# Two-block decoder on one core: weight splits ahead of the new tile's parts, and ScalarE squaring the tiles of the second block's first norm

## The chip, the cores and the metric

One core of a Trainium2 chip runs the whole program as a single launch. The metric is the device time of that launch in microseconds (us), as the median of several runs; less is better.

## The reference, cut to what matters

The reference is a decoder in fp32 for 256 tokens of width 2048: one pooling layer, one layer of sparse attention, a norm, and then a second block with three kinds of attention and a feed-forward part. What the change touches is what stands between a residual sum and the projections behind it:

```python
return x + jnp.concatenate([y_nsa, y_mem], axis=-1) @ w_out   # "wo1": x becomes the layer's output
...
x = first_block(...)            # ends with rmsnorm(h, final_g)
h = rmsnorm_2(x, attn_norm[l])  # the second block's first norm, of a tensor that has just been normed
qkv = jnp.einsum('bsd,de->bse', h, w_qkv[l])
...
x = x + jnp.einsum('bse,ed->bsd', y, w_o[l])                  # "wo2"
h = rmsnorm_2(x, ffn_norm[l])
```

The kernel takes the two norms in a row as one. For that it needs two sums over the 2048 channels of every token: of x squared, and of (x times final_g) squared.

## The kernel before, in words

Activations lie transposed: the residual `M.X` is 16 tiles (j = 0 to 15) of 128 channels by 256 tokens. Every weight is streamed once from HBM, in 699 **units** of at most 128x1024 numbers. A matmul of fp32 numbers is made of fp32r products: ScalarE rounds a unit to its high part (`s_wh`, line 1050), VectorE subtracts to get the low part (`s_wl`, line 1572), and TensorE multiplies both. These two steps are the **split** of a unit. On every engine's program `nxt()` stands for one unit: it lets the side tasks (attention heads and the like) advance by one step and then issues the split. The split of unit k+3 waits until TensorE has finished unit k (three buffers, `NR`), and SyncE loads a unit into one of four staging buffers when VectorE has split the unit four before it.

A **residual stage** is the output projection that is added to `M.X`: `wo0` (first layer), `wo1` (second layer), `wo2` (second block's attention) and `wd` twice (feed-forward). A tile of the wo stages has two units. For the first `early` tiles (4 in wo0, 8 in wo1, 12 in wo2) TensorE does the first unit of each tile, then the second unit of each, as there are late inputs; the tiles behind them have both units in a row. After each unit or tile VectorE adds the product to `M.X` (`add`, lines 1798 and 1800). When a tile is complete, `post(j)` makes its **parts** for the next matmuls: ScalarE the high part (`high`, line 1062), VectorE the low part (`low`, line 1590), and GpSimd its share of the sum of squares. GpSimd has two scratch tiles (`PSQ`) and one accumulator per sum (`ACC`).

Each engine executes its own instructions strictly in the order written here; waits are on semaphores. Behind wo1, TensorE starts the group `qc` (four tiles: their four first units, then their four second ones). Between the fourth and the fifth unit stands `eff_hook`: it waits until both sums have all 16 tiles (`sqc1`, `sqc2`) and then does the two matmuls with ones that add them over the channels (line 578). The same norm is used two more times, one unit and two units later (`eff_norms`, lines 587 and 578). ScalarE and VectorE turn the result into a reciprocal root (lines 1067, 1069 and 1596 to 1600).

GpSimd's next work behind the sums of wo1 is `late()`: eight small scalings, a cast (line 2366) that waits for the table `con3`, and an addition over 128x2048 numbers into the bias table `s_bt` (line 2370). SyncE issues the loads of both tables behind the weight unit that is eight behind the last of wo1.

Of the kernel before, what the change touches and what calls it, by code (L numbers as in the profile page):

```python
# [11 lines left out]
ALU = mybir.AluOpType  # L12
ACT = mybir.ActivationFunctionType
# [4 lines left out]
KT = 16  # L18
# [1018 lines left out]
def scalar_program(e, S, P, M):  # L1037
    w, side, done = Waits(e, S), Side(), [0]
# [13 lines left out]
    def nxt(n=1):  # L1052
        for _ in range(n):
            side.tick()
            split()
# [4 lines left out]
    def high(R, j, src, gain, name):  # L1060

        e.activation(R[:, 0, j, :], src, ACT.Copy, scale=gain).then_inc(S[name + "h"], 1)
# [221 lines left out]

    def square(n):
        w.wait_ge("l2_o", n + 1)
        w.wait_ge("z_d", 32)
        if n >= 2:
            w.wait_ge("hn_mm", n - 1)
        e.activation(M.ZT[n % 2][:, :], M.PSO[n % 2][:, 0:T], ACT.Square).then_inc(S["hn_sq"], 1)  # L1290

    def head_rsqrt(n, dim, eps):
# [112 lines left out]
    def residual(name, post, order=2, early=4, units=2):  # L1405
        for n in range(order):
            for j in range(early):
                if n == order - 1:
                    post(j)
                nxt()  # L1410
        for j in range(early, KT):
            nxt(units - 1)
            post(j)
            nxt()


    tables()
# [74 lines left out]
    def post_c(j):  # L1492
        w.wait_ge(*P.out["wo1", j])
        w.wait_ge("gfa", 1)
        w.wait_ge("units", P.end["zm", 1, 3])
        high(M.RY, j, M.X[:, j, :], M.GFA[:, j:j + 1], "hc")

    residual("wo1", post_c, early=8)

# [28 lines left out]
    for hv in range(2):  # L1528
# [14 lines left out]
        def post(j, hv=hv):  # L1543
            if hv:
                side.start(times_g(j))
# [15 lines left out]
def vector_program(e, S, P, M):  # L1561
    w, side, done, chained = Waits(e, S), Side(), [0], [0]
# [11 lines left out]
    def nxt(n=1):  # L1574
        for _ in range(n):
            side.tick()
            split()
# [33 lines left out]
    def whole(t):  # L1611
        w.wait_ge("units", P.end[t])
        return M.product(P.bank[t])
# [181 lines left out]
    def add(t, j):  # L1795

        b = whole(t)
        chain(e.tensor_tensor(M.X[:, j, :], b[:, T:2 * T], M.X[:, j, :], ALU.add))  # L1798
        link()
        e.tensor_tensor(M.X[:, j, :], b[:, 0:T], M.X[:, j, :], ALU.add).then_inc(S["out"], 1)  # L1800

    def residual(name, post, order=(0, 1), early=4, units=2, begin=None):
        for n, m in enumerate(order):
            for j in range(early):
                last = n == len(order) - 1
                if n == 0 and begin:
                    begin(j)
                if n:
                    w.wait_ge(*P.out[name, "part", order[n - 1], j])
                add((name, j) if last else (name, "part", m, j), j)  # L1810
                if last:
                    post(j)
                nxt()
        for j in range(early, KT):
            nxt(units - 1)
            if begin:
                begin(j)
            add((name, j), j)
            post(j)
            nxt()  # L1820

    def kv_norm():
        yield
# [389 lines left out]
    for hv in range(2):  # L2213
# [25 lines left out]
        def post(j, hv=hv):  # L2239
            if hv and j == KT - 1:  # L2240
                w.wait_ge(*P.out[("wd", 1), j])
                w.wait_ge("y_lo", 48)
                e.tensor_tensor(M.YT[0][:, :], M.X[:, j, :], M.X[:, j, :], ALU.mult).then_inc(S["sq15"], 1)
# [4 lines left out]
    for n, (a, b) in enumerate(((0, 1), (1, 3), (3, 6), (6, 9), (9, 11))):  # L2248
        w.wait_ge("xg", b)
        for j in range(a, b):  # L2250
            x = e.tensor_tensor(M.X[:, j, :], M.X[:, j, :], M.RB[1][:, :], ALU.mult)
# [3 lines left out]
def pool_program(e, S, P, M):  # L2255
    w, side, chained = Waits(e, S), Side(), [0]
# [6 lines left out]
    def chain(ins):  # L2263

        ins.then_inc(S["pool"], 1)
        chained[0] += 1

    def link():
        w.wait_ge("pool", chained[0])

    squared = [0]

    def square(acc, j, src, name):

        if j == 0:
            e.tensor_tensor(acc, src, src, ALU.mult).then_inc(S[name], 1)
            return
        b = M.PSQ[squared[0] % 2][:, :]
        squared[0] += 1
        chain(e.tensor_tensor(b, src, src, ALU.mult))  # L2280
        link()
        w.wait_ge(name, j)
        e.tensor_tensor(acc, acc, b, ALU.add).then_inc(S[name], 1)  # L2283
# [200 lines left out]
        side.start(mem_head(1, j))  # L2484

    def post_c(j):
        x = M.X[:, j, :]
        w.wait_ge(*P.out["wo1", j])
        if j:
            w.wait_ge("sqc2", j)  # L2490
        square(M.ACC[0][:, :], j, x, "sqc1")
        b, b2 = M.PSQ[squared[0] % 2][:, :], M.PSQ[(squared[0] + 1) % 2][:, :]
        squared[0] += 2
        chain(e.tensor_scalar(b, x, M.vec("fing", j), None, ALU.mult))  # L2494
        link()
        if j == 0:
            e.tensor_tensor(M.ACC[1][:, :], b, b, ALU.mult).then_inc(S["sqc2"], 1)
            return
        chain(e.tensor_tensor(b2, b, b, ALU.mult))
        link()  # L2500
        e.tensor_tensor(M.ACC[1][:, :], M.ACC[1][:, :], b2, ALU.add).then_inc(S["sqc2"], 1)  # L2501
    residual(post_c, early=8)


# [40 lines left out]
    for a, b in ((11, 12), (12, 14), (14, 16)):  # L2545
        w.wait_ge("xg", b)
        for j in range(a, b):
            x = e.tensor_tensor(M.X[:, j, :], M.X[:, j, :], M.RB[1][:, :], ALU.mult)
# [162 lines left out]
```

## Time and profile before

| what | value |
|---|---|
| median of 3 runs | 2118.11 us (2116.64 to 2118.48) |
| the profiled execution's own time | 2117.76 us |
| its span in the profile | 2116.0 us |
| busy: TensorE, VectorE, ScalarE, GpSimd | 98%, 69%, 48%, 24% of the span |
| mean granted clock of TensorE | 0.991 of full speed |
| moved from HBM | 365.97 MB read, 174 GB/s over the span |

In the rows further down PE is TensorE, DVE is VectorE, ACT is ScalarE, POOL is GpSimd and SPq is SyncE's DMA queue. A row of the timeline gives the start in us, the duration in us, the engine, the line of the kernel, the operation, output <- inputs with their shapes, the number of instructions merged in the row, and in brackets the idle time ahead of it with what ended it. A row of the windows gives the stretch and its length, then the busy time of PE, PE's weight loads, DVE, ACT and POOL with their counts, then the granted clock of TensorE (1.00 is 2.4 GHz, 0.50 is 1.2 GHz), the DMA share and GB/s. Line 510 is the low-part matmul of a tile's last k-step; TensorE executes it once per tile or part, always one matmul before the end of the unit, so the distance between two such rows is a number of whole units.

### The profile page before, as it was taken

Reading aid. Unit: us, or ns where it says so; the run is one execution under the profiler, and the core shown is the slowest. Engines: PE = TensorE matmul, PEld = TensorE weight load, DVE = VectorE, ACT = ScalarE, POOL = GpSimd, SP = SyncE. Lnnn points to the kernel's source line nnn. Section 1 sums busy time; section 2 is a strip of 40 time slices with the busy share of each in tenths; the row PEclk is TensorE's granted clock in tenths of the full one; section 3 lists DMA queues with packets and bytes.
Section 4 is the critical chain, followed back from the end, with each engine's and each line's share of the span. In section 5 each row is a group of like instructions: output and inputs, shape, how many; then the busy total and the mean of one; then the engine's idle time right before and its main releaser. Section 6 shows DMA issues by size and latency. Waiting matters only on the chain.

```text
span 2116.0 us, 29531 instructions
## 1 busy us (share of the span) xinstructions
PE 2063.7 (98%) x11608; PEld 1775.0 (84%) x11608; DVE 1465.3 (69%) x2054; ACT 1008.4 (48%) x1476; POOL 509.3 (24%) x487
## 2 busy tenths in 40 slices
PE   7999999999999999989999999999999999999997
PEld 6788888888888888778877888888888888888886
DVE  8866777689786556767645677677776557777755
ACT  5545444455633554433545554455444344444443
POOL 8205542200000344790221222211010001101122
PEclk9999999999999999999999999999999999999998
DMA  7564565656754333555454445565566666556664
GB/s 247 171 187 151 184 189 189 189 191 213 220 184 146 117 105 120 169 185 179 155 164 132 147 154 160 176 192 186 188 190 183 185 190 190 188 184 193 179 187 134
DMA packets 104090, 369.99 MB, mean 175 GB/s; under 512 B 11632, under 2 KB 12944, under 8 KB 103824
## 3 DMA queue, kind: packets, MB, share of 16 engines
q1 hardware_dynamic: 103952, 368.11, 55.6%
q8 instruction: 92, 1.51, 0.3%
q14 instruction: 46, 0.38, 0.1%
HBM read 365.97 MB, written 2.10 MB: 174 GB/s over the span
## 4 chain that ended last, share of the span: by engine, by line
PE 88%; DVE 5%; POOL 4%; issue 2%; ACT 1%; DMA 0%; DVEq 0%; SPq 0%; POOLq 0%; ACTq 0%
PE psg L511 47%; PE psg L513 23%; PE psg L558 2%; PE psg L560 2%; PE psg L559 2%; DVE s_wl L1572 2%; PE psg L510 2%; PE pst L511 1%; ACT s_wh L1050 1%; POOL s_psq L2494 1%; POOL s_acc L2501 1%; POOL s_psq L2280 1%; PE pst L595 1%; DVE s_rh L1590 1%; DVE s_ry L1590 1%
## 5 line engine op out<-in xcount | busy, mean ns | idle before, releaser
L1572 DVE TENSOR_TENSOR s_wl<-s_stage,s_wh 128x1024 fp32r<-128x1024 f32 (+3 forms) x699 | 870.2, 1246 | 380.7 <-ACT s_wh L1050 378.0
L1050 ACT ACTIVATE s_wh<-s_stage 128x1024 fp32r<-128x1024 f32 (+3 forms) x699 | 727.3, 1042 | 673.6 <-PE psg L511 361.7
L511 PE MATMUL psg<-s_ry,s_wh 128*128 128x512 f32 x2672 | 943.1, 398 | 3.3 <-DVE s_mv L1639 2.5
L513 PE MATMUL psg<-s_ry,s_wl 128*128 128x256 f32 x2501 | 707.6, 283 | 0.0
L511 PEld LDWEIGHTS psg<-s_ry,s_wh 128*128 128x128 f32 x2672 | 493.6, 188 | 112.2 <-issue 3.5
L511 PE MATMUL psg<-s_rh,s_wh 128*128 128x512 f32 x1280 | 460.5, 401 | 19.7 <-DVE s_rh L1590 10.5
L513 PEld LDWEIGHTS psg<-s_ry,s_wl 128*128 128x128 f32 x2501 | 471.4, 188 | 7.7
L513 PE MATMUL psg<-s_rh,s_wl 128*128 128x256 f32 x1180 | 334.6, 284 | 0.0
L511 PEld LDWEIGHTS psg<-s_rh,s_wh 128*128 128x128 f32 x1280 | 238.6, 189 | 74.6 <-issue 10.5
L511 PE MATMUL psg<-s_hid,s_wh 128*128 128x512 f32 x704 | 244.6, 394 | 0.0
L513 PEld LDWEIGHTS psg<-s_rh,s_wl 128*128 128x128 f32 x1180 | 223.6, 190 | 2.9
L2410 POOL TENSOR_TENSOR s_hid<-s_hh,s_hid 128x256 fp32r<-128x256 f32 x44 | 53.0, 1205 | 571.4 <-ACT s_hid L1395 571.4
L513 PE MATMUL psg<-s_hid,s_wl 128*128 128x256 f32 x664 | 187.4, 282 | 0.0
L511 PEld LDWEIGHTS psg<-s_hid,s_wh 128*128 128x128 f32 x704 | 129.6, 188 | 27.1
L513 PEld LDWEIGHTS psg<-s_hid,s_wl 128*128 128x128 f32 x664 | 124.8, 188 | 2.0
L2280 POOL TENSOR_TENSOR s_psq<-s_x 128x256 f32<-128x256 f32 x74 | 59.5, 805 | 167.6 <-DVE s_x L1800 165.6
L2283 POOL TENSOR_TENSOR s_acc<-s_acc,s_psq 128x256 f32<-128x256 f32 x89 | 92.5, 1039 | 7.0
L2287 POOL TENSOR_SCALAR s_bsc<-s_bsc,s_stat 128x256 f32<-128x256 f32 (+1 forms) x56 | 44.2, 805 | 194.1 <-DVE s_stat L1950 181.7
L2292 POOL TENSOR_TENSOR s_rh<-s_yt,s_rh 128x256 fp32r<-128x256 f32 x32 | 43.0, 1345 | 117.7 <-ACT s_rh L1090 117.7
L1798 DVE TENSOR_TENSOR s_x<-psg,s_x 128x256 f32<-128x256 f32 x112 | 47.3, 422 | 34.1 <-PE psg L511 33.5
L558 PE MATMUL psg<-s_wh,s_ry 128*128 128x512 f32 x160 | 65.0, 406 | 3.6 <-DVE s_kcc L1624 1.3
L2287 POOL TENSOR_SCALAR s_csc<-s_csc,s_stat 128x128 f32<-128x128 f32 (+1 forms) x32 | 34.8, 1100 | 123.5 <-DVE s_stat L1993 110.4
(388 smaller groups left out, 2268.6 us busy)
## 6 DMA issues: line engine op xcount, KB each, us to landing
s_stage<-in_wo SPq DMA_DIRECT2D x96, 512.0 KB, 3.5
s_stage<-in_wg SPq DMA_DIRECT2D x88, 512.0 KB, 3.5
s_stage<-in_wu SPq DMA_DIRECT2D x88, 512.0 KB, 3.8
s_stage<-in_ain SPq DMA_DIRECT2D x64, 512.0 KB, 3.6
s_stage<-in_wd SPq DMA_DIRECT2D x64, 448.0 KB, 3.5
s_stage<-in_wkv SPq DMA_DIRECT2D x32, 512.0 KB, 4.0
s_stage<-in_wd SPq DMA_DIRECT2D x32, 512.0 KB, 3.6
s_stage<-in_bq SPq DMA_DIRECT2D x24, 512.0 KB, 3.6
```

Of the source, the lines that this page charges most:

```text
L510: e.matmul(o[:, T:2 * T], M.WL[:, r, ws], xh, start=False, stop=False)
L511: m = e.matmul(o, M.WH[:, r, ws], xx, start=begin, stop=end)
L513: m = e.matmul(o[:, T:2 * T], M.WL[:, r, ws], xh, start=False, stop=False)
L558: e.matmul(o[:, :], xh[:, ts], M.WH[:, r, ws], start=(k == 0), stop=False)
L1050: e.activation(M.WH[:, c % NR, 0:n], M.ST[:, c % NS, 0:n], ACT.Copy).then_inc(S["wh"], 1)
L1572: e.tensor_tensor(M.WL[:, c % NR, 0:n], M.ST[:, c % NS, 0:n], M.WH[:, c % NR, 0:n], ALU.subtract).then_inc(S["wl"], 1)
L1798: chain(e.tensor_tensor(M.X[:, j, :], b[:, T:2 * T], M.X[:, j, :], ALU.add))
L2280: chain(e.tensor_tensor(b, src, src, ALU.mult))
L2283: e.tensor_tensor(acc, acc, b, ALU.add).then_inc(S[name], 1)
L2287: x = e.tensor_scalar(ap, ap, scale, None, ALU.mult)
L2292: e.tensor_tensor(R[:, 1, j, :], M.YT[y % 2][:, :], R[:, 0, j, :].bitcast(F32), ALU.subtract).then_inc(S["y_lo"], 1)
L2410: e.tensor_tensor(M.HID[:, 1, i, :], M.HH[j % 2][:, :], M.HID[:, 0, i, :].bitcast(F32), ALU.subtract).then_inc(S["hidl"], 1)
```

## The change

Two edits. First, in the residual stages the split of a unit now comes ahead of `post(j)` on ScalarE and on VectorE: in the early zone `nxt()` then `post(j)`; behind it ScalarE does both splits and then the parts, and VectorE does split, add, split, parts. Second, in wo1 ScalarE makes both squares of a tile (into `PSQ` and into `ZT`, two buffers each) right behind the high part, and GpSimd only adds them to the two accumulators.

```diff
     # ScalarE's program
     def residual(name, post, order=2, early=4, units=2):
         for n in range(order):
             for j in range(early):
+                nxt()
                 if n == order - 1:
                     post(j)
-                nxt()
         for j in range(early, KT):
-            nxt(units - 1)
+            nxt(units)
             post(j)
-            nxt()
...
     def post_c(j):
...
         high(M.RY, j, M.X[:, j, :], M.GFA[:, j:j + 1], "hc")
+        w.wait_ge("sqk", KT)
+        w.wait_ge("z_d", 32)
+        if j >= 2:
+            w.wait_ge("sqc1", j - 1)
+            w.wait_ge("sqc2", j - 1)
+        e.activation(M.PSQ[j % 2][:, :], M.X[:, j, :], ACT.Square).then_inc(S["sqp"], 1)
+        e.activation(M.ZT[j % 2][:, :], M.X[:, j, :], ACT.Square, scale=M.vec("fing", j)).then_inc(S["sqg"], 1)
...
     # VectorE's program, residual()
                 add((name, j) if last else (name, "part", m, j), j)
+                nxt()
                 if last:
                     post(j)
-                nxt()
...
             add((name, j), j)
+            nxt()
             post(j)
-            nxt()
...
     # GpSimd's program
     def post_c(j):
-        x = M.X[:, j, :]
-        w.wait_ge(*P.out["wo1", j])
-        if j:
-            w.wait_ge("sqc2", j)
-        square(M.ACC[0][:, :], j, x, "sqc1")
-        b, b2 = M.PSQ[squared[0] % 2][:, :], M.PSQ[(squared[0] + 1) % 2][:, :]
-        squared[0] += 2
-        chain(e.tensor_scalar(b, x, M.vec("fing", j), None, ALU.mult))
-        link()
-        if j == 0:
-            e.tensor_tensor(M.ACC[1][:, :], b, b, ALU.mult).then_inc(S["sqc2"], 1)
-            return
-        chain(e.tensor_tensor(b2, b, b, ALU.mult))
-        link()
-        e.tensor_tensor(M.ACC[1][:, :], M.ACC[1][:, :], b2, ALU.add).then_inc(S["sqc2"], 1)
+
+        for acc, src, made, name in ((M.ACC[0], M.PSQ, "sqp", "sqc1"), (M.ACC[1], M.ZT, "sqg", "sqc2")):
+            w.wait_ge(made, j + 1)
+            if j == 0:
+                e.tensor_copy(acc[:, :], src[0][:, :]).then_inc(S[name], 1)
+            else:
+                w.wait_ge(name, j)
+                e.tensor_tensor(acc[:, :], acc[:, :], src[j % 2][:, :], ALU.add).then_inc(S[name], 1)
```

How the instructions now stand, at three places. The changed file has other line numbers on VectorE and GpSimd: 1572 is 1579 there, 1590 is 1597, 1798 and 1800 are 1805 and 1807.

VectorE in wo1, at the first tile that is complete, before:

```order
L1798 TENSOR_TENSOR s_x<-psg,s_x 128x256
L1800 TENSOR_TENSOR s_x<-psg,s_x 128x256
L1590 SCALAR_TENSOR_TENSOR s_ry<-s_x,s_gfa,s_ry 128x256
L1572 TENSOR_TENSOR s_wl<-s_stage,s_wh 128x1024
L1798 TENSOR_TENSOR s_x<-psg,s_x 128x256
```

The same place in the changed kernel:

```order
L1805 TENSOR_TENSOR s_x<-psg,s_x 128x256
L1807 TENSOR_TENSOR s_x<-psg,s_x 128x256
L1579 TENSOR_TENSOR s_wl<-s_stage,s_wh 128x1024
L1597 SCALAR_TENSOR_TENSOR s_ry<-s_x,s_gfa,s_ry 128x256
L1805 TENSOR_TENSOR s_x<-psg,s_x 128x256
```

The split (output `s_wl`) has moved from behind the low part (output `s_ry`) to between the addition and the low part. The pattern repeats for each early tile, and is the same in wo0 and wo2.

ScalarE in wo1 at the first complete tiles, before:

```order
L1090 ACTIVATE s_rh<-s_yt 128x256
L1050 ACTIVATE s_wh<-s_stage 128x1024 x2
L1062 ACTIVATE s_ry<-s_x,s_gfa 128x256
L1050 ACTIVATE s_wh<-s_stage 128x1024
L1062 ACTIVATE s_ry<-s_x,s_gfa 128x256
```

And in the changed kernel:

```order
L1090 ACTIVATE s_rh<-s_yt 128x256
L1050 ACTIVATE s_wh<-s_stage 128x1024 x3
L1062 ACTIVATE s_ry<-s_x,s_gfa 128x256
L1502 ACTIVATE s_psq<-s_x 128x256
L1503 ACTIVATE s_zt<-s_x,s_vec 128x256
L1050 ACTIVATE s_wh<-s_stage 128x1024
L1062 ACTIVATE s_ry<-s_x,s_gfa 128x256
```

One more split (output `s_wh`) stands ahead of the first high part, and two squares (lines 1502 and 1503) follow each high part. No table load is added on ScalarE.

GpSimd in wo1, its work for one tile, before:

```order
L2280 TENSOR_TENSOR s_psq<-s_x 128x256
L2283 TENSOR_TENSOR s_acc<-s_acc,s_psq 128x256
L2494 TENSOR_SCALAR s_psq<-s_x,s_vec 128x256
L2499 TENSOR_TENSOR s_psq<-s_psq 128x256
L2501 TENSOR_TENSOR s_acc<-s_acc,s_psq 128x256
```

In the changed kernel, its first three tiles:

```order
L2498 COPY s_acc<-s_psq 128x256
L2498 COPY s_acc<-s_zt 128x256
L2501 TENSOR_TENSOR s_acc<-s_acc,s_psq 128x256
L2501 TENSOR_TENSOR s_acc<-s_acc,s_zt 128x256
L2501 TENSOR_TENSOR s_acc<-s_acc,s_psq 128x256
L2501 TENSOR_TENSOR s_acc<-s_acc,s_zt 128x256
```

Five instructions per tile became two.

## Rows read from the trace of the kernel before

**Rows 1.** The page: busy time of each engine.

```profile
PE 2063.7 (98%) x11608; PEld 1775.0 (84%) x11608; DVE 1465.3 (69%) x2054; ACT 1008.4 (48%) x1476; POOL 509.3 (24%) x487
```

**Rows 2.** Timeline of PE, line 510: wo0, wo1, behind its hook, wo2.

```profile
339.94 0.27 PE L510 MATMUL psg<-s_ry,s_wl 128*128 128x256 f32 x1
...
357.50 0.28 PE L510 MATMUL psg<-s_ry,s_wl 128*128 128x256 f32 x1
...
865.29 0.27 PE L510 MATMUL psg<-s_rh,s_wl 128*128 128x256 f32 x1
...
895.07 0.28 PE L510 MATMUL psg<-s_rh,s_wl 128*128 128x256 f32 x1
...
923.17 0.28 PE L510 MATMUL psg<-s_rh,s_wl 128*128 128x256 f32 x1
...
948.28 0.27 PE L510 MATMUL psg<-s_ry,s_wl 128*128 128x256 f32 x1
...
951.97 0.28 PE L510 MATMUL psg<-s_ry,s_wl 128*128 128x256 f32 x1
...
955.21 0.27 PE L510 MATMUL pst<-s_ry,s_wl 128*128 128x256 f32 x1
...
1298.46 0.27 PE L510 MATMUL psg<-s_rh,s_wl 128*128 128x256 f32 x1
...
1358.41 0.28 PE L510 MATMUL psg<-s_rh,s_wl 128*128 128x256 f32 x1
```

**Rows 3.** Timeline of DVE: one early tile of wo2.

```profile
1303.08 0.42 DVE L1800 TENSOR_TENSOR s_x<-psg,s_x 128x256 f32<-128x256 f32 x1
1304.08 0.49 DVE L1590 SCALAR_TENSOR_TENSOR s_ry<-s_x,s_vec,s_ry 128x256 fp32r<-128x256 f32 x1 [0.58 <-ACT s_ry L1062]
1305.03 1.23 DVE L1572 TENSOR_TENSOR s_wl<-s_stage,s_wh 128x1024 fp32r<-128x1024 f32 x1 [0.46 <-ACT s_wh L1050]
...
1306.62 0.42 DVE L1800 TENSOR_TENSOR s_x<-psg,s_x 128x256 f32<-128x256 f32 x1
```

**Rows 4.** Timeline of ACT: the same tile.

```profile
1303.54 0.51 ACT L1062 ACTIVATE s_ry<-s_x,s_vec 128x256 fp32r<-128x256 f32 x1 [2.09 <-DVE s_x L1800]
1303.95 1.04 ACT L1050 ACTIVATE s_wh<-s_stage 128x1024 fp32r<-128x1024 f32 x1
```

**Rows 5.** Timeline of POOL in wo1: its first, one middle and its last instruction.

```profile
855.62 0.61 POOL L2276 TENSOR_TENSOR s_acc<-s_x 128x256 f32<-128x256 f32 x1 [7.30 <-DVE s_x L1800]
...
920.98 1.59 POOL L2501 TENSOR_TENSOR s_acc<-s_acc,s_psq 128x256 f32<-128x256 f32 x1
...
942.00 0.72 POOL L2501 TENSOR_TENSOR s_acc<-s_acc,s_psq 128x256 f32<-128x256 f32 x1
```

**Rows 6.** Timeline of PE: the first matmul of the hook behind wo1.

```profile
942.83 1.19 PE L578 MATMUL pso<-s_acc,s_one 128*128 128x256 f32 x2 [7.91 <-issue]
```

**Rows 7.** Windows, behind an early wait and behind the hook's wait.

```profile
70.20:73.30 3.10, 3.10 (x12) 2.62 (x11) 1.67 (x6) 0.00 (x0) 0.00 (x0) 0.50 0.76 276
942.80:947.20 4.40, 4.37 (x12) 3.65 (x13) 1.26 (x4) 1.84 (x3) 4.15 (x9) 0.50 0.01 3
```

**Rows 8.** Waits of PE: us in total, times, longest; two of them.

```profile
PE psg L511 <- DVE s_mv L1639: 2.5, 1, 2.5
...
PE psg L558 <- DVE s_kcc L1624: 1.3, 1, 1.3
```

**Rows 9.** Timeline of SPq, POOL and DVE behind the hook: table and bias addition.

```profile
933.07 0.43 SPq L2591 DMA_DIRECT2D s_csc<-in_con  x1
...
947.13 1.55 DVE L1572 TENSOR_TENSOR s_wl<-s_stage,s_wh 128x1024 fp32r<-128x1024 f32 x1
...
947.57 5.56 POOL L2370 TENSOR_TENSOR s_bt<-s_bt,s_csc 128x2048 f32<-128x2048 f32 x1
...
949.62 3.79 DVE L1626 SCALAR_TENSOR_TENSOR s_qc<-s_qc,s_rb 128x256 f32<-128x256 f32 x1
```

**Rows 10.** DMA issues of that stretch: KB each, median us to landing.

```profile
s_csc<-in_con SPq DMA_DIRECT2D x1, 320.0 KB, 9.1
```

More of the change, by code:

```diff
@@ L1286, in square @@
         w.wait_ge("l2_o", n + 1)
-        w.wait_ge("z_d", 32)
         if n >= 2:
             w.wait_ge("hn_mm", n - 1)
+        else:
+            w.wait_ge("sqc2", KT)
         e.activation(M.ZT[n % 2][:, :], M.PSO[n % 2][:, 0:T], ACT.Square).then_inc(S["hn_sq"], 1)
@@ L2486, in post_c @@
     def post_c(j):
-        x = M.X[:, j, :]
-        w.wait_ge(*P.out["wo1", j])
-        if j:
-            w.wait_ge("sqc2", j)
-        square(M.ACC[0][:, :], j, x, "sqc1")
-        b, b2 = M.PSQ[squared[0] % 2][:, :], M.PSQ[(squared[0] + 1) % 2][:, :]
-        squared[0] += 2
-        chain(e.tensor_scalar(b, x, M.vec("fing", j), None, ALU.mult))
-        link()
-        if j == 0:
-            e.tensor_tensor(M.ACC[1][:, :], b, b, ALU.mult).then_inc(S["sqc2"], 1)
-            return
-        chain(e.tensor_tensor(b2, b, b, ALU.mult))
-        link()
-        e.tensor_tensor(M.ACC[1][:, :], M.ACC[1][:, :], b2, ALU.add).then_inc(S["sqc2"], 1)
+        for acc, src, made, name in ((M.ACC[0], M.PSQ, "sqp", "sqc1"), (M.ACC[1], M.ZT, "sqg", "sqc2")):
+            w.wait_ge(made, j + 1)
+            if j == 0:
+                e.tensor_copy(acc[:, :], src[0][:, :]).then_inc(S[name], 1)
+            else:
+                w.wait_ge(name, j)
+                e.tensor_tensor(acc[:, :], acc[:, :], src[j % 2][:, :], ALU.add).then_inc(S[name], 1)
     residual(post_c, early=8)
```

## The prediction

> **What bounds the kernel now.** I read the page first: TensorE is busy for 98% of the span, VectorE for 69%, GpSimd for 24% [rows 1]. So only what makes TensorE wait, or run slowly, can be won back, and the page alone hides it, because a matmul that is held up is stretched in the records and counts as busy. I therefore measured TensorE by the distance between its line-510 matmuls, which is a whole number of units. At its own pace a unit takes 2.81 us: from 895.07 to 923.17 are 10 units, 28.10 us [rows 2]. Against that ruler four places are late:
>
> - wo0, 339.94 to 357.50: 6 units, 17.56 us instead of 16.86, late by 0.70.
> - wo1, 865.29 to 895.07: 9 units, 29.78 instead of 25.29, late by 4.49.
> - wo2, 1298.46 to 1358.41: 19 units, 59.95 instead of 53.39, late by 6.56.
> - the hook behind wo1, 923.17 to 948.28: 5 units (14.05) and the hook's two matmuls. One such matmul costs 0.43: 951.97 to 955.21 is 3.24, a unit and one matmul. So 14.91 would do, 25.11 were taken: late by 10.20 [rows 2].
>
> The timelines say why. In an early tile VectorE adds (two instructions), sits idle 0.58 for ScalarE's high part, does the low part, sits idle 0.46 for the split that ScalarE did only behind the high part, and splits. A tile comes every 3.54 us (1303.08 to 1306.62), although VectorE works only 0.42 + 0.42 + 0.49 + 1.23 = 2.56 of it [rows 3]. ScalarE spends 2.09 idle and 1.55 busy [rows 4]. It is a ring of waits, with no engine full. The splits are some units ahead when a zone begins, which is worth 1.5 us: in wo2 eleven intervals of 3.54 exceed TensorE's by 11 x 0.73 = 8.0, and 6.56 were lost.
>
> The hook is another matter. GpSimd needs from 855.62 to 942.72 for the sums of 16 tiles, 5.4 us each, with an instruction of 0.61 to 0.72 alone and up to 1.59 in company [rows 5], while a tile leaves TensorE every 2.81 or 5.62. It ends 0.1 us ahead of the hook's first matmul, which had waited 7.91 [rows 6]. And behind that idle time the granted clock is 0.50, its 1.2 GHz level, for 4.40 us [rows 7]: half of these, 2.2, is the rest of the 10.20.
>
> **The change part by part.**
>
> 1. Split ahead of the parts. VectorE's order becomes add, split, low. ScalarE's split now waits only for TensorE, and runs while VectorE adds; the high part runs while VectorE splits. Both idle times of the ring close, and VectorE's work of 2.56 per early tile fits under 2.81. TensorE is the bound again. What is later by it are the parts, by one split (1.23) at most; they are for the group behind the stage, whose second half needs the last of them more than 11 us (four units) later, so this costs nothing. Saved: 0.70 + 4.49 + 6.56 = 11.75. At wd TensorE keeps its pace, and only ScalarE's final scalings move by a unit: 0.
>
> 2. ScalarE's squares. Not in the trace in this form; the nearest row is the high part, same shape and engine, 0.51 [rows 4]. Per early tile of wo1: 1.04 + 3 x 0.51 = 2.57, below 2.81; later tiles 3.6 of 5.62. The bounds: 0.4 and 0.6 each give 2.4 and 2.8, both fit. I take 0. If they did not fit, each 0.1 over would cost 8 x 0.1, less the 1.5 of lead. Behind the waiting square on ScalarE stands the split of the next unit, for which VectorE and then TensorE wait.
>
> 3. GpSimd's two additions. 0.72 each alone, 1.59 each in company [rows 5]: 1.4 to 3.2 per tile where it was 5.4. At 3.2 it falls behind the 2.81 of the early tiles by 0.4 x 7 = 2.8, and two buffers and the 5.62 tiles take that in. After the last tile it needs one high part, two squares and two additions, some 4 to 5 us; the hook stands four units, 11.2 us, behind. The wait is gone with 6 us to spare, and with it the slow clock. Saved: 10.20.
>
> 4. What is late next. With GpSimd free early, its bias addition runs as soon as its tables are there. The split that releases the table's load comes 4.49 earlier: issue 933.07 - 4.49 = 928.6, landing 9.1 later [rows 9, 10], 937.7; the cast some 0.5, so the addition starts at 938.2. It shows 5.56, of which its start, 947.57 to 948.68, lies under a split of VectorE: 4.45 alone. A VectorE instruction with two inputs from the same memory stood through it: 3.79 where its like takes 0.49 [rows 3, 9]. Before, that fell into the time that TensorE's stall had given away. Now: the hook starts at about 934.8 - 4.5 = 930.3. Until the fifth unit behind it, TensorE has 0.86 of the hook, four units (11.24), 0.88 for the column sums (948.28 to 951.97 less a unit) and 0.43 [rows 2]: it wants that unit at 943.7. VectorE is held until 938.2 + 4.45 = 942.7, then has the rest of its instruction (0.3), three small ones (0.42 each) and the split (1.23) [rows 3] and a signal of 0.1 to 0.2: 945.7. Wait: 2.0. Is the clock halved behind that? Behind the wait of 2.5 it was 0.50 for the 3.10 us of the window, behind those of 1.3 nothing is late [rows 7, 8]; 2.0 is nearer to 2.5, so I add half of 3.1, 1.6. Bounds: 0 (the table lands when VectorE can spare it) and 5.56 + 2.2. I take 3.6.
>
> The sum: 11.75 + 10.20 - 3.6 = 18.35. The profiled execution took 2117.76 (span 2116.0): 2099.4. It stands 0.35 below the median, so I say **2099.8**, 0.86% less.
>
> **A price for the memory port.** The row that shows a cost is the 3.79 [rows 9]. The Trainium skill, "SBUF — State Buffer", section "SBUF: two separate sides", says that VectorE with two SBUF inputs and a GpSimd instruction that reads SBUF exclude each other for a whole instruction. By that rule, which speaks against closing the ring, the time is that of rival B, 2101.1, since splits and low parts could not overlap GpSimd at all; by the rows alone it is 2099.8.
>
> **The rivals.**
>
> - A, the bias addition costs nothing: it lands in spare time, or VectorE is further ahead than I have it. For it: TensorE runs from 951.97 to 955.21 with no loss right under the 3.79. Against it: there it had been given 10 us. Time 2118.1 - 21.95 = 2096.2.
> - B, VectorE and GpSimd take turns in the early zones. Split, low part, square and addition do not overlap: 1.23 + 0.49 + 0.61 + 0.72 = 3.05 per tile [rows 3, 5], 0.24 over TensorE's. In wo2 11 x 0.24 = 2.6 less the lead of 1.5 costs 1.1, in wo1 0.2. For it: an addition of 1.59. Against it: VectorE's additions from the product take 0.84 per tile in which GpSimd can have the memory, and the lead grows as the split is earlier. Time 2101.1; with a longer wait at the bias addition up to 2104.5.
> - C, the ring closes only in part, because the parts or the additions hold the product's buffers and so TensorE: half of the 11.75 remains, 2105.7.
> - D, slower: the handshake on wo1's two square buffers. ScalarE's square of tile j waits for GpSimd's additions of tile j-2, and its splits stand behind. If GpSimd took P per tile, TensorE would be paced by P. The gain of 18.35 and 4.2 more are eaten if 16 tiles take 22.6 + 1.5 longer than the 67.4 of their 24 units: P above 5.7, so 2.9 per addition where the longest row has 1.59. Time 2122 at that point. That the change does nothing is excluded by the orders of instructions; the same time would need P about 5.4.
>
> **How the numbers follow.** The forecast (2097.5 to 2101.5) 0.45; A 0.23; B and a dearer bias addition 0.22; C 0.05; D and no change 0.05. From 2095.3, a little below A, to 2104.5, the end of B, lie 0.88 less what spills over the edges. What tells a change here from none is 0.2%, 4.2 us; only D and the edge of C are not faster: faster 0.94, same 0.03, slower 0.03.
>
> **What would show it.** Step 1: line-510 distances of 2.81 or 5.62 throughout wo0, wo1 and wo2, and VectorE's additions 2.81 apart. Step 2: squares of 0.4 to 0.6, no long idle time of ScalarE ended by GpSimd. Step 3: GpSimd's last addition of wo1 some 5 us behind the last tile, no idle time at the first line-578 matmul, clock 1.00 there. Step 4: a VectorE instruction of 3 to 4.5 us under the bias addition and a TensorE gap of about 2 us within four to six units of the hook. The prediction is wrong if line-510 distances stay above 2.9 in the early zones, if ScalarE waits for GpSimd tile after tile, or if a new stall appears behind wo1 that the profile before has no sign of.

## The result and the profile after

The changed kernel takes **2096.06 us** (median of 4 runs, 2095.16 to 2096.87), beside 2117.41 (4 runs, 2116.64 to 2118.48) for the kernel before on the same chip: ratio 0.9901, 95% interval 0.9889 to 0.9912. The forecast was 2099.8 with a range of 2095.3 to 2104.5. The profiled execution took 2095.29 us, its span is 2093.5 us.

The page after, busy time of each engine, to be read against [rows 1]:

```profile
PE 2056.4 (98%) x11608; PEld 1771.4 (85%) x11608; DVE 1482.3 (71%) x2054; ACT 1022.6 (49%) x1508; POOL 483.1 (23%) x441
```

ScalarE has 32 more instructions and GpSimd 46 fewer; TensorE's share still says nothing. The ruler does. Line 510 of TensorE in the changed kernel, in wo1 and in wo2, where [rows 2] were late by 4.49 and 6.56:

```profile
865.20 0.27 PE L510 MATMUL psg<-s_rh,s_wl 128*128 128x256 f32 x1
870.82 0.27 PE L510 MATMUL psg<-s_rh,s_wl 128*128 128x256 f32 x1
...
915.78 0.28 PE L510 MATMUL psg<-s_rh,s_wl 128*128 128x256 f32 x1
...
1296.54 0.27 PE L510 MATMUL psg<-s_rh,s_wl 128*128 128x256 f32 x1
...
1313.42 0.27 PE L510 MATMUL psg<-s_rh,s_wl 128*128 128x256 f32 x1
```

From 865.20 to 915.78 are 18 units in 50.58 us, from 1296.54 to 1313.42 six units in 16.88: 2.81 each, and so through all of wo0, wo1 and wo2. The ring is gone. VectorE, ScalarE and GpSimd at one early tile of wo2, to be read against [rows 3, 4]:

```profile
1305.77 0.41 DVE L1805 TENSOR_TENSOR s_x<-psg,s_x 128x256 f32<-128x256 f32 x1
...
1306.68 1.23 DVE L1579 TENSOR_TENSOR s_wl<-s_stage,s_wh 128x1024 fp32r<-128x1024 f32 x1
1307.82 0.83 DVE L1597 SCALAR_TENSOR_TENSOR s_ry<-s_x,s_vec,s_ry 128x256 fp32r<-128x256 f32 x1
1308.58 0.41 DVE L1805 TENSOR_TENSOR s_x<-psg,s_x 128x256 f32<-128x256 f32 x1
```
```profile
1308.40 1.06 ACT L1050 ACTIVATE s_wh<-s_stage 128x1024 fp32r<-128x1024 f32 x1 [1.22 <-PE psg L511]
```
```profile
1306.72 1.66 POOL L2287 TENSOR_TENSOR s_psq<-s_x 128x256 f32<-128x256 f32 x1 [0.27 <-DVE s_x L1807]
```

VectorE's additions stand 2.81 apart (1305.77, 1308.58), and ScalarE's split waits for TensorE and for nothing else. VectorE has no idle time left in these rows. GpSimd's square begins beside VectorE's split (1306.72 and 1306.68) and takes 1.66, where its like takes 0.61 alone; the low part behind the split takes 0.83, where it was 0.49. The two engines hold each other up, and since VectorE's additions still keep TensorE's 2.81, there is just room for it.

The hook behind wo1 [rows 6]: TensorE's rows from the last of wo1 to the end of the late places, GpSimd's last sum and its next work, and VectorE under the bias addition.

```profile
927.37 0.59 PE L578 MATMUL pso<-s_acc,s_one 128*128 128x256 f32 x2
...
930.68 0.28 PE L510 MATMUL psg<-s_ry,s_wl 128*128 128x256 f32 x1
...
937.62 0.27 PE L510 MATMUL pst<-s_ry,s_wl 128*128 128x256 f32 x1
...
939.07 0.51 PE L511 MATMUL pst<-s_ry,s_wh 128*128 128x512 f32 x1 [0.94 <-DVE s_wl L1579]
...
941.63 0.28 PE L510 MATMUL pst<-s_ry,s_wl 128*128 128x256 f32 x1
...
942.61 0.47 PE L511 MATMUL psg<-s_ry,s_wh 128*128 128x512 f32 x1 [0.47 <-DVE s_wl L1579]
...
947.96 0.28 PE L510 MATMUL psg<-s_ry,s_wl 128*128 128x256 f32 x1
```
```profile
919.28 0.92 POOL L2501 TENSOR_TENSOR s_acc<-s_acc,s_zt 128x256 f32<-128x256 f32 x1
920.18 5.74 POOL L2368 TENSOR_SCALAR s_ids<-s_cons 128x128 bf16<-128x128 f32 x8
932.63 0.66 POOL L2373 CAST s_ddb<-s_csc 128x384 bf16<-128x384 f32 x1 [6.71 <-DMA s_csc<-in_con]
933.26 4.60 POOL L2377 TENSOR_TENSOR s_bt<-s_bt,s_csc 128x2048 f32<-128x2048 f32 x1
```
```profile
933.34 4.54 DVE L1607 SCALAR_TENSOR_TENSOR s_rc<-s_cw,s_rc 128x2 f32<-128x2 f32 x1
937.80 1.21 DVE L1579 TENSOR_TENSOR s_wl<-s_stage,s_wh 128x1024 fp32r<-128x1024 f32 x1
```

From 915.78 to 930.68 are 14.90 us where 25.11 were, and the first matmul at line 578 has no idle time ahead of it; GpSimd was done at 920.20, 7.2 us before. Then TensorE is late by 1.20 (937.62 to 941.63, less 2.81) and 0.71 (941.63 to 947.96, less 5.62): 1.91. The reason is the row of VectorE at 933.34: an instruction over two columns stands for 4.54 us, as long as GpSimd's bias addition beside it. The windows behind the hook and over the waits:

```profile
927.00:931.00 4.00, 4.00 (x24) 3.55 (x23) 1.69 (x5) 2.02 (x4) 0.00 (x0) 1.00 1.02 424
938.00:946.00 8.00, 6.59 (x36) 5.47 (x36) 7.83 (x13) 2.36 (x3) 0.00 (x0) 1.00 0.40 131
```

The granted clock is 1.00 in both.

**Where the 22.5 us between the two profiled executions are.** wo0 0.70, wo1 4.47, wo2 6.52, the hook 10.21, the waits behind it -1.61 (1.91 now, where the kernel before lost 0.30 at the same unit), a place in the first layer 1.6, the start-up 0.6. The place in the first layer is none of the change's. It is a group of 48 matmuls of 15 columns; its row and the window around it, before and then after:

```profile
656.44 6.57 PE L736 MATMUL pss<-s_kcmp,s_qn 128*128 128x15 f32 x48
```
```profile
655.00:672.00 17.00, 17.00 (x99) 15.58 (x98) 10.65 (x26) 3.78 (x5) 0.00 (x0) 0.80 0.34 100
```
```profile
655.12 5.51 PE L736 MATMUL pss<-s_kcmp,s_qn 128*128 128x15 f32 x48
```
```profile
655.00:672.00 17.00, 17.00 (x107) 15.47 (x106) 10.64 (x25) 4.84 (x6) 0.00 (x0) 0.90 0.44 130
```

The clock falls to half in every profiled execution around this group though TensorE never idles there, and for longer in some: 0.90 of 17 us is 3.4 us at half clock, 0.80 is 6.8, which is 1.7 or 3.4 us of lost work. The kernels below show the same at the same code: 0.90 in the profiled runs of e1, e6, e7, e9 and e11, 0.80 in those of e2, e3, e4, e8 and e10, and 0.70, 10.2 us at half clock, in that of e5. Runs of one kernel differ by about as much: the changed kernel's four are two of 2095.2 to 2095.3 with a mean clock of 0.996 and two of 2096.8 to 2096.9 with 0.994.

### The profile page after: what moved, and what is told of

The parts are those of the page before. It is cut to its first block, busy times and chain, and to the rows that moved or that the text cites. A ratio compares the mean times of both kernels' runs of the same rounds, so it can differ in the third digit from the quotient of the medians.

```text
span 2093.5 us, 29532 instructions
## 1 busy us (share of the span) xinstructions
PE 2056.4 (98%) x11608; PEld 1771.4 (85%) x11608; DVE 1482.3 (71%) x2054; ACT 1022.6 (49%) x1508; POOL 483.1 (23%) x441
## 4 chain that ended last, share of the span: by engine, by line
PE 94%; DVE 4%; issue 0%; ACT 0%; DMA 0%; DVEq 0%; SPq 0%; ACTq 0%
PE psg L511 51%; PE psg L513 25%; PE psg L558 2%; PE psg L560 2%; PE psg L559 2%; PE psg L510 2%; DVE s_wl L1579 2%; PE pst L511 1%; PE pst L595 1%; DVE s_rh L1597 1%; PE pst L513 1%; DVE s_ry L1597 1%; PE pss L759 1%; PE pso L779 0%; PE pst L683 0%; PE pst L684 0%
## 5 line engine op out<-in xcount | busy, mean ns | idle before, releaser
L2290 POOL TENSOR_TENSOR s_acc<-s_acc,s_psq 128x256 f32<-128x256 f32 x74 | 85.8, 1160 | 5.8
```

## The experiments

All are compared with the kernel before, run on the same chip (median 2116.5 to 2117.7). "Interval" is the distance of two line-510 matmuls in an early zone. The change has one more edit than the two that are told above: the tiles `ZT` also serve ScalarE's later squares of the heads, and the first two of those now wait for the sums of wo1 (`sqc2`) instead of `z_d`. e1 is without it, all the others have it; in the trace of the changed kernel no wait of ScalarE at those squares is ended by GpSimd.

**e1, the new order alone.** The kernel before with the diff's first part only; GpSimd does all five instructions per tile.

```diff
 # VectorE, residual(), against before (ScalarE likewise); both post_c as before
+                nxt()
                 if last:
                     post(j)
-                nxt()
... (and the same behind the early tiles)
```

> The kernel before with the new order of split and parts alone; GpSimd still makes both squares of wo1. My theory (two waits in series): wo0 gives back 0.7 us and wo2 6.6 us, but the 4.5 us won in wo1 are lost again at the hook, because GpSimd's chain of 5.4 us per tile ends at the same time whatever TensorE does; the idle time at the first line-578 matmul grows from 7.9 to about 12 us. Total 2117.4 - 7.3 = 2110.1 us. Rival (the savings simply add): 2117.4 - 11.75 = 2105.7 us.

Measured 2105.19 us (2104.52 to 2106.59), ratio 0.9944 (0.9927 to 0.9960). My 2110.1 was wrong and the additive rival's 2105.7 nearly right. The zones run at 2.81. The hook, which I had supposed to wait for all that TensorE gains ahead of it, waits only 1 us more than before. TensorE, and then GpSimd in e1 and in the kernel before:

```profile
936.12 1.19 PE L578 MATMUL pso<-s_acc,s_one 128*128 128x256 f32 x2 [8.90 <-issue]
```
```profile
931.34 0.72 POOL L2500 TENSOR_TENSOR s_acc<-s_acc,s_psq 128x256 f32<-128x256 f32 x1
...
935.29 0.72 POOL L2500 TENSOR_TENSOR s_acc<-s_acc,s_psq 128x256 f32<-128x256 f32 x1
```
```profile
938.05 0.72 POOL L2501 TENSOR_TENSOR s_acc<-s_acc,s_psq 128x256 f32<-128x256 f32 x1
```

GpSimd's chain started earlier with TensorE, and it became faster too: from its first instruction (852.39) to 936.0 are 83.6 us where it was 87.1 [rows 5], 5.2 per tile instead of 5.4. The pace of a tile isn't fixed. The last one takes 3.95 us in both kernels (931.34 to 935.29; before, 938.05 to 942.00 [rows 5]), while most of those behind the early zone take 5.6 in both. Of the 3.5 us gained, 1.8 lie in the last three tiles: 5.6, 4.0 and 4.0 in e1, 6.7, 4.8 and 4.0 before. The likely reason is that VectorE's work for wo1 is over at an earlier tile of GpSimd's; no run isolates it.

**e2, the squares alone.** The changed kernel with both engines' old order.

```diff
 # ScalarE, residual(), against the changed kernel (VectorE likewise)
-                nxt()
                 if n == order - 1:
                     post(j)
+                nxt()
...
-            nxt(units)
+            nxt(units - 1)
             post(j)
+            nxt()
```

> The changed kernel with the old order of split and parts, so that only the squares have moved to ScalarE. My theory: the wait at the hook and the slow clock go (10.2 us), the bias addition costs 1.6 of it, and the ring of waits in wo1 becomes longer by the two squares that now stand between the high part and the split on ScalarE (0.7 us per early tile, 7 tiles, 4.9 us): 2117.4 - 10.2 + 1.6 + 4.9 = 2113.7 us; the interval of VectorE's additions in wo1's early zone goes from 3.55 to about 4.25 us. Rival (savings simply add, the ring stays at 3.55): 2108.8 us.

Measured 2113.16 us (10 runs, 2111.7 to 2114.1), ratio 0.9981 (0.9972 to 0.9990): as I expected, and not the 2108.8 of the additive rival. In wo1 TensorE is paced at 4.25 us per tile, slower than before:

```profile
866.44 0.28 PE L510 MATMUL psg<-s_rh,s_wl 128*128 128x256 f32 x1
870.68 0.28 PE L510 MATMUL psg<-s_rh,s_wl 128*128 128x256 f32 x1
```
```profile
870.32 1.23 DVE L1580 TENSOR_TENSOR s_wl<-s_stage,s_wh 128x1024 fp32r<-128x1024 f32 x1 [1.17 <-ACT s_wh L1050]
```

VectorE now idles 1.17 ahead of its split where it was 0.46 [rows 3]: the squares lengthen the ring by 0.71, since ScalarE's split stands behind them. So the squares are hidden in the changed kernel only because the split stands ahead of them; together the two edits give more than their sum, 21.4 us where e1 has 12.3 and e2 4.3. Behind the hook TensorE waited once, for 1.64 us, and the clock stayed at 1.00.

**e4, only ScalarE's order** (VectorE keeps add, low, split; squares as in the changed kernel).

```diff
 # VectorE, residual(), against the changed kernel
-                nxt()
                 if last:
                     post(j)
+                nxt()
... (and the same behind the early tiles)
```

> The changed kernel with VectorE's old order (add, low part, split); ScalarE keeps split, high part, squares. My theory: the ring of waits is half open: VectorE waits 0.2 to 0.6 us per early tile for the high part and not for the split, an interval of about 2.9 to 3.1 us against TensorE's 2.81; less the lead this costs 0 to 2 us in wo2 and about 0.5 us in wo1: 2096 to 2098.5 us. Rival (only VectorE's order matters, since the split must reach TensorE through it): the early zones fall back to 3.5 us per tile, 2107 us.

Measured 2106.10 us (2105.17 to 2108.49), ratio 0.9947 (0.9933 to 0.9962). My 2096 to 2098.5 was wrong; the rival's number, 2107, held, but not its reason, that only VectorE's order matters: e5 below has VectorE's new order alone and is slower still. The interval is 3.53, although ScalarE's split is done in time. Against e2, which has neither engine's new order, that is still 7.1 us less. VectorE in wo2:

```profile
1309.22 0.48 DVE L1597 SCALAR_TENSOR_TENSOR s_ry<-s_x,s_vec,s_ry 128x256 fp32r<-128x256 f32 x1 [0.58 <-ACT s_ry L1062]
1309.62 1.76 DVE L1579 TENSOR_TENSOR s_wl<-s_stage,s_wh 128x1024 fp32r<-128x1024 f32 x1
```

Of the two idle times the 0.46 is gone, but the split now takes 1.76 instead of 1.23. GpSimd's addition stands beside its start. That is 0.53 given back in another form, which raised the question that the next run answers.

**e9, the same without GpSimd in wo2.** The kernel leaves out the sum of squares behind wo2.

```diff
-        square(M.ACC[0][:, :], j, M.X[:, j, :], "sqf")
+        if j == 0:
+            square(M.ACC[0][:, :], j, M.X[:, j, :], "sqf")
+        else:
+            w.wait_ge("sqf", j)
+            e.tensor_tensor(M.ACC[0][:, 0:2], M.ACC[0][:, 0:2], M.X[:, j, 0:2], ALU.add).then_inc(S["sqf"], 1)
```

> ScalarE's new order alone, VectorE's old one (add, low, split), and in wo2 GpSimd's square and addition of 128x256 numbers per tile replaced by one addition of 128x2 from the second tile on (so that the sum of squares behind wo2, and with it the output, is left out). With full squares this order gave an interval of 3.54 us, and VectorE's split took 1.76 us instead of 1.23 while GpSimd added. My theory: those 0.53 us are VectorE waiting for the memory that GpSimd holds; without GpSimd the interval in wo2 is 0.42 + 0.42 + 0.58 idle + 0.49 + 1.23, less some overlap, 3.0 us, wo2 loses some 0.8 us instead of 6.56, and the time is 2106.1 - 5.8 = 2100.3 us; wo1 stays at 3.53. Rival: the split is held by something of ScalarE or TensorE, and GpSimd only stands beside it: the interval stays 3.54 and the time 2106.

Measured 2100.85 us (2098.87 to 2102.92), ratio 0.9924 (0.9911 to 0.9938), 5.3 less than e4 where I had said 5.8.

```profile
1308.88 0.49 DVE L1597 SCALAR_TENSOR_TENSOR s_ry<-s_x,s_vec,s_ry 128x256 fp32r<-128x256 f32 x1 [0.58 <-ACT s_ry L1062]
1309.28 1.22 DVE L1579 TENSOR_TENSOR s_wl<-s_stage,s_wh 128x1024 fp32r<-128x1024 f32 x1
...
1311.87 0.48 DVE L1597 SCALAR_TENSOR_TENSOR s_ry<-s_x,s_vec,s_ry 128x256 fp32r<-128x256 f32 x1 [0.58 <-ACT s_ry L1062]
```

The split is back at 1.22, and the low parts stand 2.99 apart instead of 3.53. So the 0.53 were VectorE waiting for the memory that GpSimd held. The interval of 2.9 to 3.1 that I had expected of e4 is there once GpSimd is out of the way, and the lead nearly covers it: TensorE's matmuls stay 2.81 apart in wo2 until the last early tile and lose 0.3 us in all.

**e5, only VectorE's order** (ScalarE keeps parts, then split).

```diff
 # ScalarE, residual(), against the changed kernel
-                nxt()
                 if n == order - 1:
                     post(j)
+                nxt()
... (and the same behind the early tiles)
```

> The changed kernel with ScalarE's old order (high part, squares, split); VectorE keeps add, split, low part. My theory: the ring is longer than in the kernel before, as VectorE's split now waits for the addition, the high part and ScalarE's split in series and the low part stands behind it: 0.85 + 0.45 + 1.05 + 1.2 + 0.4 = about 4.0 us per early tile in wo0 and wo2 and 4.7 us in wo1. Loss against the changed kernel: wo2 11 x 1.2 - 1.5 = 11.6, wo1 7 x 1.9 - 1.5 = 11.8, wo0 3 x 1.2 - 1.5 = 2.1: about 2121 us, slower than the kernel before. Rival (the order on either engine gives half of the gain): 2107 us.

Measured 2123.47 us (8 runs, 2121.89 to 2125.02), ratio 1.0028 (1.0018 to 1.0039): slower than before, as expected. Interval 3.94 in wo0 and wo2, 4.64 in wo1 (I had 4.0 and 4.7). VectorE in wo2:

```profile
1308.29 1.23 DVE L1580 TENSOR_TENSOR s_wl<-s_stage,s_wh 128x1024 fp32r<-128x1024 f32 x1 [1.53 <-ACT s_wh L1050]
```

This half of the edit makes a longer ring: add, high part, split, VectorE's split, add.

**e6, one square ahead instead of two.**

```diff
-            w.wait_ge("sqc1", j - 1)
-            w.wait_ge("sqc2", j - 1)
+            w.wait_ge("sqc1", j)
+            w.wait_ge("sqc2", j)
```

> The changed kernel in which ScalarE's squares of tile j wait for GpSimd's additions of tile j-1, as if there were one buffer of each kind. My theory: GpSimd's additions end 0.6 us ahead of the next tile's square, so the handshake has room and nothing changes, 2096.1 us. Rival (the handshake is near its limit, and the second buffer is what hides it): ScalarE waits in the early zone, up to 0.5 us per tile less the lead, 2098 us or more.

Measured 2095.60 us (2094.89 to 2097.07), ratio 0.9901: no change. Rival D's handshake has room even at half its depth.

**e7, GpSimd's work doubled in wo1.**

```diff
                 w.wait_ge(name, j)
+                spare = M.ET[0 if name == "sqc1" else 1]
+                e.tensor_tensor(spare[:, :], src[j % 2][:, :], src[j % 2][:, :], ALU.add)
                 e.tensor_tensor(acc[:, :], acc[:, :], src[j % 2][:, :], ALU.add).then_inc(S[name], 1)
```

> The changed kernel with two more additions of the same kind by GpSimd for each tile of wo1 from the second one on (into a scratch tile that nobody reads), four instead of two. My theory: GpSimd's time per tile goes from 1.7 to 3.7 to 4.6 us, over TensorE's 2.81 in the early zone, and through the two buffers it paces ScalarE and so TensorE there; 7 x 0.9 to 1.8 less two buffers and the lead is a loss of 2 to 7 us: 2098 to 2103 us. Rival (VectorE waits for GpSimd instruction by instruction, and the time is lost there): VectorE's interval rises with every GpSimd instruction also in the later tiles, 2105 us or more. Third: GpSimd is off the path at any load that fits 5.62 us, 2096.1 us.

Measured 2095.61 us (2095.01 to 2095.93), ratio 0.9899: no change, where I had 2098 to 2103. ScalarE does wait for GpSimd, at the seventh tile for the first time:

```profile
873.32 0.42 ACT L1502 ACTIVATE s_psq<-s_x 128x256 f32<-128x256 f32 x1 [1.61 <-POOL s_acc L2503]
```

VectorE's additions are 3.0 to 3.1 apart, some 0.25 over TensorE's pace, and TensorE lost 0.14 us in all: seven tiles of 0.24 are 1.7, and the splits that were ahead took nearly all of it. That is the interval of rival B, measured in wo1, where B had priced it at 0.2. In wo2, with its eleven intervals, no run has it.

**e3, the bias addition in four pieces of 128x512.**

```diff
-        e.tensor_tensor(M.BT[:, :, :], M.BT[:, :, :], chm, ALU.add).then_inc(S["bt"], 1)
+        for q in range(4):
+            b = M.BT[:, 2 * q:2 * q + 2, :]
+            x = e.tensor_tensor(b, b, chm[:, 2 * q:2 * q + 2, :], ALU.add)
+        x.then_inc(S["bt"], 1)
```

> The changed kernel with GpSimd's bias addition over 128x2048 done in four pieces of 128x512. My theory: VectorE stood 4.5 us behind the one long instruction because GpSimd holds what both need for a whole instruction; with pieces of about 1.2 us VectorE gets in between them, the low part of the unit comes in time and the two TensorE gaps behind the hook (1.9 us together against TensorE's own pace) go: 2096.1 - 1.9 = 2094.2 us. Rival (the total that GpSimd holds it decides, not the length of one piece): VectorE is as late as before, 2096.1 us.

Measured 2095.36 us (2094.32 to 2096.73), ratio 0.9898 (0.9883 to 0.9913). VectorE at the same instruction:

```profile
933.74 1.23 DVE L1607 SCALAR_TENSOR_TENSOR s_rc<-s_cw,s_rc 128x2 f32<-128x2 f32 x1
```

It is held for one piece (1.23 instead of 4.54) and then gets in between. TensorE is late by 0.60 instead of 1.91, where I had expected nothing to be left; the 1.3 us are seen in the trace, while the median lies between my 2094.2 and the rival's 2096.1 and, 0.7 from the changed kernel's, doesn't separate the two.

**e8, the tables loaded four units earlier.** What the addition costs should depend on when it runs.

```diff
-    while issued[0] < P.end["wo1", KT - 1] + 9:
+    while issued[0] < P.end["wo1", KT - 1] + 5:
```

> The whole change, but SyncE issues the tables' loads four units (11.2 us) earlier, so that GpSimd's cast and bias addition need no longer wait for them: they start behind its eight scalings, at about 926 to 927 us instead of 933. My theory: the 1.91 us that TensorE is late behind the hook come from the moment at which the bias addition holds VectorE; at 927 VectorE is still ahead of TensorE by its full lead, the distances behind the hook become 14.90, 3.69, 3.24, 2.81 and 5.62, and the time is 2096.06 - 1.9 = 2094.2 us. Rival 1: the addition of 4.6 us takes from VectorE what it takes at any moment, and TensorE is late by 1.9 us all the same, only at another unit: 2096. Rival 2: the addition now holds the column sums and reciprocal roots behind the hook, which TensorE waits for, and more is lost: 2098.

Measured 2094.69 us (2093.81 to 2095.13), ratio 0.9893 (0.9879 to 0.9906), the fastest kernel of the study. GpSimd, VectorE and TensorE:

```profile
928.10 5.55 POOL L2377 TENSOR_TENSOR s_bt<-s_bt,s_csc 128x2048 f32<-128x2048 f32 x1
```
```profile
931.60 2.33 DVE L1605 SCALAR_TENSOR_TENSOR s_nw<-s_nw,s_rb 128x256 f32<-128x256 f32 x1
```
```profile
931.00:938.00 7.00, 7.00 (x45) 6.26 (x44) 6.68 (x10) 3.33 (x8) 2.65 (x1) 1.00 0.32 109
```

The addition now starts 5.2 us earlier in the trace, and 6.9 earlier against TensorE's matmuls of the hook. Its start lies under a split of VectorE, 1.94 us of it in a time in which VectorE waits for ScalarE, and only 1.9 are left for the instruction at 931.60. The distances behind the hook are 14.90, 3.69, 3.24, 2.81 and 5.62: nothing is late. The profiled run gained the 1.9 though it drew the longer half clock at line 736. The wait hung on the moment, as my theory had it, and both rivals are out by the distances. The medians are 1.4 apart, less than the 1.7 between runs of the changed kernel; the 1.9 rest on the trace.

**e10 and e11, the bias addition held longer.** They ask whether a longer wait at this place brings the half clock that the prediction charged, the step of it that failed.

```diff
+        held = M.BT[:, 0:4, :]      # e10; in e11 0:8, the whole table
+        chain(e.tensor_tensor(held, held, chm[:, 0:4, :], ALU.add))
+        link()
         e.tensor_tensor(M.BT[:, :, :], M.BT[:, :, :], chm, ALU.add).then_inc(S["bt"], 1)
```

> The whole change, with GpSimd's bias addition preceded by one more addition over half of the same table (128x1024, so that this half gets its mask twice). In the changed kernel the addition held VectorE for 4.60 us and TensorE was late by 1.91 us in two waits, the longer 0.94, with the clock at 1.00 behind them, where I had forecast a wait of 2.0 and half a clock. This makes the wait longer by 2.3 to 2.8. My theory (a longer wait does bring the half clock that the prediction charged, as behind the waits of 2.5 and 7.91 before): TensorE is late by 1.9 + 2.5 = 4.4 and the window behind it shows 0.50 for some 3 us, 1.5 more, 5.9 in all; time 2096.1 + 4.0 = 2100.1 us. Rival (behind the hook the clock does not fall for such waits): late by 4.4, clock 1.00, time 2098.6.

> The same with the additional addition over the whole table (128x2048, all of it gets its mask twice). My theory: TensorE is late by 1.9 + 4.6 to 5.0 = 6.6 to 6.9, then the clock is 0.50 for 3 to 4.4 us, 1.5 to 2.2 more: 8.4 in all, time 2096.1 + 6.5 = 2102.6 us. Rival (clock stays 1.00): late by 6.7, time 2100.9. Second rival: VectorE slips its splits in between the two additions and less than 5 is lost in all, time below 2099.

e10 took 2099.04 us (2098.2 to 2099.89), ratio 0.9917 (0.9903 to 0.9932); e11 2101.43 (2100.5 to 2103.51), ratio 0.9932 (0.9915 to 0.9948). Both lie between my numbers (2100.1, 2102.6) and the rival's (2098.6, 2100.9); the trace decides. TensorE's one wait in e10, and the windows behind it:

```profile
944.43 0.59 PE L511 MATMUL psg<-s_ry,s_wh 128*128 128x512 f32 x1 [3.16 <-DVE s_wl L1579]
```
```profile
944.00:946.00 2.00, 1.57 (x5) 1.40 (x6) 1.97 (x5) 0.00 (x0) 0.00 (x0) 0.66 0.30 109
946.00:948.00 2.00, 2.00 (x7) 1.64 (x7) 1.97 (x4) 0.00 (x0) 0.00 (x0) 0.50 0.46 166
```

Behind 3.16 us of waiting, TensorE runs at its 1.2 GHz level until 948. Between two line-510 matmuls that are two units apart lie 10.57 us there: 4.95 late, of which 1.8 are the half clock. e11 has waits of 0.95 and 4.14, then 0.50 again (948 to 950), and is late by 1.19 + 5.91 = 7.10. So a half clock of the size charged can follow at this place, in the one profiled execution of each; the wait was shorter than I had it (3.16 for 4.4), since VectorE does a split between the two additions.

They don't make a rule of the length. The program has a wait of 1.8 us near 31 us that the change doesn't touch. TensorE's row and the window around it, in the kernel before and in the changed one, and then in e10 the wait of 2.5 that the prediction leaned on [rows 8]:

```profile
31.17 0.50 PE L511 MATMUL psg<-s_rh,s_wh 128*128 128x512 f32 x1 [1.81 <-DVE s_wl L1572]
```
```profile
28.00:36.00 8.00, 6.08 (x25) 4.73 (x24) 8.00 (x8) 1.73 (x3) 7.68 (x9) 0.79 0.57 188
```
```profile
30.37 0.50 PE L511 MATMUL psg<-s_rh,s_wh 128*128 128x512 f32 x1 [1.79 <-DVE s_wl L1579]
```
```profile
28.00:36.00 8.00, 6.21 (x35) 5.22 (x35) 8.00 (x8) 2.92 (x4) 7.68 (x8) 1.00 0.58 197
```
```profile
68.88 0.50 PE L511 MATMUL psg<-s_ry,s_wh 128*128 128x512 f32 x1 [2.46 <-DVE s_mv L1646]
```
```profile
66.00:74.00 8.00, 5.54 (x31) 4.52 (x30) 6.92 (x11) 3.88 (x6) 3.28 (x4) 1.00 0.58 200
```

0.79 of 8 us is 3.4 us at half clock, 1.00 is none. Of the 13 profiled executions six have the half clock at the wait of 1.8 (before, e1, e3, e4, e5, e8), and ten have it at the wait of 2.5 (all but e3, e4 and e10). The same wait of the same code is followed by it in one execution and not in another.

## Why the prediction was right, step by step

The measured 2096.06 lies in the range of 2095.3 to 2104.5, but outside the forecast's own band of 2097.5 to 2101.5: the range holds it because rival A set its lower end.

**Step 1, split ahead of the parts: right, in mechanism and size.** 11.75 forecast, 11.69 measured, with VectorE's additions 2.81 apart. One engine's new order alone gives 3.53 (e4) or 3.94 (e5), so beside GpSimd's work both idle times had to go; e9 shows that without that work ScalarE's order alone would nearly do, at 2.99. VectorE's time per tile isn't the 2.56 that the prediction reckoned with but all of 2.81, since GpSimd holds it for 0.34 of them. What the prediction left open is by which wait the ring held TensorE. In the kernel before, all eight gaps of TensorE in the early zone of wo2 are of this kind:

```profile
1310.65 0.51 PE L511 MATMUL psg<-s_rh,s_wh 128*128 128x512 f32 x1 [0.45 <-DVE s_x L1800]
```

They end with VectorE's addition, which frees one of the two buffers of the product (`psg`), and not with a split. That buffer is what rival C was about; with the additions 2.81 apart it holds nothing.

**Step 2, ScalarE's squares for nothing: right.** They take 0.40 and 0.49, so an early tile costs ScalarE 2.46 where the sum had 2.57. e2 shows what the cover was worth: without the new order they cost 0.71 per tile.

**Step 3, GpSimd's two additions: right.** 10.20 forecast, 10.21 measured. They take 0.80 to 1.07 each; the time to spare was 7.2 us instead of 6.

**Step 4, the bias addition: right in place and cause, too dear by 2.** I had 3.6: a wait of 2.0 and half of 3.1 us at the slow clock. Four things differ.

- The waits come to 1.91, so that part was sized rightly, if partly by luck: the table landed sooner (issued at 925.80, cast at 932.63, 6.8 us later instead of 9.1), and the addition held VectorE from 933.3, at an earlier unit than I thought.
- The half clock didn't come. This is the step that failed: "2.0 is nearer to 2.5, so I add half of 3.1, 1.6", a clock read off the length of a wait. Behind the hook the clock stayed at 1.00 in all seven profiled executions whose longest wait there is 0.94 to 1.64 (the changed kernel, e2, e4, e5, e6, e7 and e9), and fell behind 3.16 and 4.14 (e10, e11). Nor does the length alone decide, as the waits of 1.8 and 2.5 show. The prediction leaned on one row, and passed over the wait of 1.81 with half a clock behind it in the same trace. (Behind the waits of 1.3 the clock is indeed 1.00, though rows 7 and 8 don't show it.) What decides beside the length stays open.
- I had one wait at one unit. It came as two, late by 1.20 and 0.71, with idle gaps of 0.94 and 0.47 and 3.1 us of matmuls between them. Whether the clock would have fallen behind one wait of 2.0 at this place, no run shows.
- The kernel before lost 0.30 at that unit, which I hadn't subtracted.

Priced so, the term is 1.6, and the sum 11.75 + 10.20 - 1.6 = 20.35 gives 2097.4 for the profiled execution, which took 2095.29. The remaining 2.1 are the 1.6 at line 736 and 0.6 of start-up, which are not of the change. The first differs between executions of the same code, as shown above; for the second no run tells what it comes from.

**The rivals.** A (2096.2) has the nearest number and the wrong reason: the bias addition was not free, it cost 1.6, and the line-736 clock gave that back; e8 is what A looks like. B's contention is there in every tile, but GpSimd's addition (1308.46 to 1309.27) lies under VectorE's two additions from the product (1308.58, 1309.03), as the argument against B had it, and only its square holds the low part, by 0.34. That makes 2.8 us of VectorE per tile, and not 3.05. At 3.05, in e7 and in wo1 alone, the price was 0.14. C and D did not occur; e7 shows that even doubled additions do not make D, and e6 that half the buffers don't.

The rule of the Trainium skill that led to B's time ("SBUF — State Buffer", section "SBUF: two separate sides": whoever starts first keeps the pair of ports that VectorE and GpSimd share for the whole instruction) is borne out by the rows: 4.54 us for two columns, and 1.23 in e3, where a piece is a quarter as long. It failed as a price, not as a rule: what counts is how much of the one engine's work falls where the other doesn't want the pair.

The two parts do not add up (e1, e2): the squares cost nothing only under the cover of the earlier split, as step 2 reckoned.

## What to carry to other kernels

When two in-order engines hand tiles to each other, write down for one tile who waits for whom; moving the independent work ahead of the dependent one gave its whole gain only when it was moved on both engines of the ring; on VectorE alone it made the ring longer (3.94 for 3.54), on ScalarE alone what it gained in wo2 went to GpSimd's hold. A long GpSimd instruction can cost VectorE its whole length, even where VectorE's next instruction is short: put it where VectorE idles anyway, or cut it. And don't add a slow clock to a wait because one row shows it behind a wait of that length: look at the same wait in several executions first.

## What the runs showed of the hardware that I hadn't expected

- A VectorE instruction over 128x2, 0.16 us otherwise, took 4.54 us beside GpSimd's 128x2048 addition of 4.60, and 1.23 beside a quarter of it (e3): the length of the holding instruction counted, not the size of the held one. VectorE's additions from the product took their usual 0.41 beside a GpSimd addition (1308.58).
- The same wait of TensorE, 1.8 us near 31 us, is followed by 3.4 us at half clock in the kernel before and by none in the changed one; the wait of 2.5 has a half clock behind it in ten of 13 executions.
- TensorE's clock fell to half around 48 matmuls of 15 columns with no idle time, for 3.4, 6.8 or 10.2 us from one execution to the next (windows of 0.90, 0.80 and 0.70). A step of 3.4, 1.7 us of work, is as large as the spread between runs of the changed kernel.
- The same chain of five GpSimd instructions took 5.4 us per tile in the mean of the kernel before and 3.95 in its last tile.
- The same table load landed 6.8 us after its issue in the changed kernel and in e8, and 9.1 before: a landing time read in one place is only an estimate for another.
